# Products of constants that nobody reads, placed on TensorE in its waits at block ends and block heads

## The reference, cut to what matters

```python
# layer 1: state space and gated linear attention, then a gated MLP (2816 hidden)
x = x + ssd_gla_layer(rms_norm(x, ...), w_in, ..., w_out)
x = x + swiglu(rms_norm(x, ...), w_gate, w_up, w_down)
# layer 2: latent attention, then a gated MLP
x = x + mla_layer(rms_norm(x, ...), ...)
x = x + swiglu(rms_norm(x, ...), ...)
# layer 3: hgrn2_mix and retention_mix over one projection, gates, then the experts
x = x + merged @ w_out
x = x + peer_ffn(rmsnorm(x, ...), w_q, sub_keys, expert_u, expert_v)   # 16384 experts
return rmsnorm(x, final_norm_w)
```

## Time and profile before

| | us |
|---|---|
| median of 3 runs | 3814.06 (3812.29 to 3815.13) |
| the profiled execution's own time | 3814.17 |
| its span, first to last instruction | 3812.3 |
| PE busy | 3602.6, 94% of the span |
| DVE, POOL, ACT busy | 1951.2, 1615.7, 1392.0 |
| mean granted clock of PE | 0.974 of full speed |

### The profile page before, as it was taken

How to read it: one execution, slowest core, us unless ns; L and a number is a source line. 1 busy time by engine, 2 the same in 40 slices (tenths; PEclk the granted TensorE clock), 3 DMA queues, 4 the chain that set the end, 5 groups by cost and what they waited for, 6 DMA issues and landing times. The chain is left out here.

```text
span 3812.3 us, 50272 instructions
## 1 busy us (share of the span) xinstructions
PE 3602.6 (94%) x17241; PEld 2991.6 (78%) x17241; DVE 1951.2 (51%) x3519; ACT 1392.0 (37%) x2156; POOL 1615.7 (42%) x838
## 2 busy tenths in 40 slices
PE   8899899998999999998899999999999999999998
PEld 6667678786677878787687777779999999788886
DVE  6724333204552330127516122358899991787886
ACT  3333332224553222221211332333348994333334
POOL 4344354344205434441243344445786776422221
PEclk9999999999999999999999999999999999999999
DMA  5123133222003322220123122234878997999996
GB/s 164 39 81 94 39 95 98 87 95 93 23 18 94 99 89 92 83 92 24 40 93 95 55 83 81 86 102 139 266 242 292 379 383 265 365 361 348 343 343 229
DMA packets 274589, 580.13 MB, mean 152 GB/s; under 512 B 119648, under 2 KB 153824, under 8 KB 273040
## 3 DMA queue, kind: packets, MB, share of 16 engines
q1 hardware_dynamic: 237584, 444.07, 35.4%
q0 software_dynamic: 36864, 134.23, 10.1%
HBM read 523.66 MB, written 54.56 MB: 152 GB/s over the span
## 5 line engine op out<-in xcount | busy, mean ns | idle before, releaser
L425 PE MATMUL ps<-h_hi,w_hi 128*128 128x512 f32 x1880 | 752.3, 400 | 59.1 <-DVE h_lo L355 31.5
L426 PE MATMUL ps<-h_lo,w_hi 128*128 128x512 f32 x1880 | 743.3, 395 | 0.0
L427 PE MATMUL ps<-h_hi,w_lo 128*128 128x512 f32 x1880 | 742.4, 395 | 0.0
L572 POOL TENSOR_TENSOR w_lo<-ring,w_hi 128x1024 fp32r<-128x1024 f32 (+1 forms) x172 | 443.9, 2581 | 659.1 <-ACT w_hi L537 659.1
L425 PEld LDWEIGHTS ps<-h_hi,w_hi 128*128 128x128 f32 x1880 | 359.8, 191 | 157.4 <-issue 45.5
L537 ACT CAST w_hi<-ring 128x1024 fp32r<-128x1024 f32 (+1 forms) x172 | 191.1, 1111 | 743.1 <-PE ps L427 718.7
L426 PEld LDWEIGHTS ps<-h_lo,w_hi 128*128 128x128 f32 x1880 | 360.6, 192 | 75.5 <-issue 2.2
L427 PEld LDWEIGHTS ps<-h_hi,w_lo 128*128 128x128 f32 x1880 | 360.0, 191 | 76.2
L3305 POOL TENSOR_TENSOR w_lo<-ring,w_hi 128x1024 fp32r<-128x1024 f32 x142 | 359.0, 2532 | 141.2 <-ACT w_hi L3180 139.9
L3180 ACT CAST w_hi<-ring 128x1024 fp32r<-128x1024 f32 x270 | 283.1, 1049 | 371.1 <-PE ps L427 305.5
L3356 PE MATMUL ps<-h_hi,w_hi 128*128 128x384 f32 (+1 forms) x1152 | 401.9, 349 | 7.6 <-DVE h_lo L355 6.1
(11 more groups left out here) (424 smaller groups left out, 6748.5 us busy)
## 6 DMA issues: line engine op xcount, KB each, us to landing
ring<-in_expert_u SPq DMA_DIRECT2D x128, 512.0 KB
ring<-in_expert_v SPq DMA_DIRECT2D x128, 512.0 KB
ring<-in_w_gate_up SPq DMA_DIRECT2D x88, 512.0 KB
acts<-expert_gelu SPq DMA_DIRECT2D x128, 192.0 KB
gates<-peer_region SPq DMA_DIRECT2D x48, 512.0 KB
peer_region<-acts SPq DMA_DIRECT2D x128, 192.0 KB
peer_region<-gates SPq DMA_DIRECT2D x128, 192.0 KB
ring<-in_w_down SPq DMA_DIRECT2D x32, 704.0 KB
```

Of the source, the lines that this page charges most:

```text
L425: pe.matmul(out, w_hi, x_hi, start=start, stop=False)
L426: pe.matmul(out, w_hi, x_lo, start=False, stop=False)
L427: return pe.matmul(out, w_lo, x_hi, start=False, stop=stop)
L572: pool.tensor_tensor(half(c.w_lo, s), raw(s), half(c.w_hi, s).bitcast(F32), ALU.subtract).then_inc(c.lo_done.sem, 1)
```

## The change

A helper `occupy` issues n products of the constant table: the unit matrix stationary, the three constants (384 columns) moving, plain float32, into a PSUM bank that is free. Nothing reads what they write. They stand in 25 places, 82 products in all: at the head of a `linear` whose first piece waits for its input, at the end of four `linear` blocks (`rest`), at the end of `linear_tokens` and of the MLP's first block, at the head of the MLP, of the latent attention and of the expert block, ahead of the last sum of squares in the gated linear attention, and at three waits of the expert block. Where the bank could still be in use, a wait on `bank_free` or on a copy stands ahead of them, and in the expert block the wait for `chosen_made` moves behind two other waits and the products.

```diff
+def occupy(c, pe, bank, n):
+    for _ in range(n):
+        pe.matmul(c.ps[:, bank, 0:3 * P], c.ident, c.basic[:, 0:3 * P], start=True, stop=True)
...
             if src or normal:
+                pe.wait_ge(c.bank_free.sem, c.bank_free.at(1))
+                occupy(c, pe, 0, 3)
                 one(0, 0, 0, 0, 0, first=True)
             pieces(one, None if root_of or more else pe.Fori, 1 if src or normal else 0)
+            if rest:
+                pe.wait_ge(c.bank_free.sem, c.bank_free.at(1 + nb))
+                occupy(c, pe, nb % 2, rest)
             if root_of:
...
             pieces(one, pe.Fori)
+            pe.wait_ge(c.bank_free.sem, c.bank_free.at(1 + nb * NCH))
+            occupy(c, pe, 0, 3)
...
                     if h:
                         sum_squares(h - 1)
+                occupy(c, pe, 3, 4)
                 sum_squares(H - 1)
...
-        linear(c, d["w_small"], DT, 1, hh, hl, low_rank, then=first_pieces(d["w_ssd"][8:20]),
+        linear(c, d["w_small"], DT, 1, hh, hl, low_rank, then=first_pieces(d["w_ssd"][8:20]), rest=4,
                normal=lambda k: c.col("mix_norm_even", k), width=0)
...
-                               more=(state.sync, state.tensor, None))
+                               more=(state.sync, state.tensor, None), rest=3)
...
                     pe.wait_ge(c.bank_free.sem, c.bank_free.at(1))
+                    occupy(c, pe, 0, 3)
                     for k in range(DT):
                         normal.ready(pe, k)
...
                     with pe.Fori(1, pairs) as p:
                         for m in range(4):
                             piece(p, m)
+                    pe.wait_ge(c.bank_free.sem, c.bank_free.at(1 + HT))
+                    occupy(c, pe, 0, 3)
...
                 def first_latents():
+                    occupy(c, pe, 0, 3)
                     pe.wait_ge(c.lo_done.sem, split_at(0))
...
-                       more=(lambda sp, m: None, gated.tensor, gated.gpsimd), then=first_pieces(d["w_branch_ret0"]))
+                       more=(lambda sp, m: None, gated.tensor, gated.gpsimd), then=first_pieces(d["w_branch_ret0"]),
+                       rest=4)
...
-            linear(c, d["w_gates"], DT, 16, hh, hl, qk, beside=(merge.vector, merge.scalar), then=first_pieces(d["w_out_2"]))
+            linear(c, d["w_gates"], DT, 16, hh, hl, qk, beside=(merge.vector, merge.scalar), then=first_pieces(d["w_out_2"]),
+                   rest=4)
...
                 def gates(g):
+                    if g == 0:
+                        occupy(c, pe, 3, 3)
                     pe.wait_ge(hot_low_made.sem, hot_low_made.at(g + 1))
...
+                occupy(c, pe, 0, 3)
                 for m in range(NQ):
...
-                pe.wait_ge(chosen_made.sem, chosen_made.at(1))
                 pe.wait_ge(scores_kept.sem, scores_kept.at(NQ))
                 pe.wait_ge(x_kept.sem, x_kept.at(8))
+                occupy(c, pe, 2, 3)
+                pe.wait_ge(chosen_made.sem, chosen_made.at(1))
...
+                occupy(c, pe, SUM_BANK[0], 6)
                 for i in range(4):
                     add(i, i, first=i == 0)
```

More of the change, by code:

```diff
@@ L430, in linear, with linear_block @@
 def linear(c, w, kt, nb, hi, lo, dst, add=False, src=None, then=None, beside=None, root_of=None, normal=None,
-           width=D, more=None, ends=None, loads=()):
+           width=D, more=None, ends=None, loads=(), rest=0):
     with ExitStack() as ctx:
         linear_block(c, ctx, w, kt, nb, hi, lo, dst, add, src, then, beside, root_of,
-                     Normal(c, ctx, normal, width, None, ends, (hi, lo)) if normal else None, more, loads)
-def linear_block(c, ctx, w, kt, nb, hi, lo, dst, add, src, then, beside, root_of, normal, more, extra=()):
+                     Normal(c, ctx, normal, width, None, ends, (hi, lo)) if normal else None, more, loads, rest)
+def linear_block(c, ctx, w, kt, nb, hi, lo, dst, add, src, then, beside, root_of, normal, more, extra=(), rest=0):
     np_ = 1 if kt <= DT else 2
```

## The result

| | before | the change |
|---|---|---|
| median, us | 3814.06 (3812.08 to 3817.4, 5 runs) | 3793.12 (3790.42 to 3799.98, 5 runs) |
| ratio, 95% interval | | 0.9948 (0.9936 to 0.996) |
| profiled execution, its span | 3814.17, 3812.3 | 3792.65, 3790.9 |
| mean granted clock | 0.974 | 0.988 |

The change is faster by 20.9 us, 0.55%. The page's busy times answer to the earlier trace rows: PE has 164 records more and is busy 24.9 us longer, in a span that is 21.4 us shorter.

What follows compares the result with a forecast made beforehand. The prediction took TensorE, slowed by a low clock behind its waits, to bound the kernel: 3814.2 - 20.0 (eight places) - 1.5 (MLP heads) + 4.0 (new falls) = 3796.7 us, range 3780 to 3811, the forecast's own 3788 to 3804.

Steps and rivals of the forecast that it cites:

- What bounds the kernel: TensorE, busy in 94% of the span; its clock falls to 0.50 behind waits, losing half the busy time there.
- What the fill costs: All 82 products: 53 us of PE, 0.324 us per record, hidden in the waits; at full clock costed at nothing.
- rival (d): Slower: head fills at low clock end 1.61 us late; twelve heads 19.3 us, 3833, or half of them 3824; chance 0.09.
- The eight places: Eight low stretches behind filled one-piece waits, followed by dense streams: half of PE's busy time each, 20.0 us gained.
- The final sum: At the sum's head, 5.3 us of wait against 3.89 of fill; gain 5.30/2 = 2.65 us.
- Heads: Block heads with two waits, only the first filled: 1.5 us for the two MLP heads together, nothing for the others.
- Rival (a): The clock holds at heads too, behind six second waits: 13.9 us more, 33.9 us less in all, 3780; chance 0.07.
- Against: Falls that newly come at unfilled waits or reach further into dense work at heads: 4 us taken off the gain.
- The sum: The forecast total: 3814.2 - 20.0 - 1.5 + 4.0 = 3796.7 us, 0.45% less.
- Rival (c): Products with the unit matrix stationary don't count for the clock; it falls as before, fill hidden: 3814; chance 0.09.
- Rival (b): Half a hold: idle time left still brings falls in part of the eight; three holding gives 7.5 us, 3807; chance 0.15.

Runs made afterwards that it cites:

- e3: The change with fill products over only 16 of the 128 rows, same number and columns: 3810.34 us, ratio 0.9994.
- e8: The change with stationary data of 16 columns instead of 128 in every fill, all 128 rows: 3794.72 us, ratio 0.9953.
- e5: The change with six products instead of three at each of the twelve block heads: 3791.41 us, ratio 0.9947.
- e9_inner: The change plus fills in the heads' second waits and at three more places in or ending the latent attention block: 3788.12 us, ratio 0.9939.
- e1: The change without the 12 fills at block heads, the 13 others kept: 3797.2 us, ratio 0.9962.
- e4: The change plus fills of two to four products in the second waits of the heads: 3792.36 us, ratio 0.995.
- e6: The change with each fill cut (three products become one, four two, six three): 3804.13 us, ratio 0.9974.

## Why the prediction was right, and where it wasn't

- **What bounds the kernel**: right. The time is lost in PE's low clock behind waits. e3 and e8 are the proof: the same number of products at the same places, and stages gain where the clock held and not where it fell, at eight of eight places with 16 columns and at three (and half of a fourth) with 16 rows.
- **What the fill costs**: right in the change, nothing, at 0.30 us from record to record (3.65 us for twelve) where I had 0.324. But the reason at heads was too narrow. I had PE late by 1.61 us if the fill outlasts the first operand, and everything behind late too. e5 shows the second wait takes it up. With this rival (d) falls as priced. Fills did run at the low clock at three heads (3.14 us to the first triple at the first MLP's), and the stage behind gained 1.2 us all the same. Only with more products at such a head did the low clock cost something, 1.1 us in e5's first MLP and 1.8 in e9_inner's against the change.
- **The eight places**: the mechanism right at all eight, the size a fifth too large, 15.9 for 20.0. "Half of the busy time" holds where PE alone sets the pace: retention 1.47 for 1.51, w_down 2.74 for 3.03, final sum 2.25 for 2.65. It fails where PE at full clock runs into the next operand. In w_ssd's two parts and in w_out_2 PE now waits 0.77, 0.45 and 0.65 us for POOL's low half of a weight, and in the gate matrices 0.40 and 0.43 more for one-hot rows. There the lead grew by 3.1 us right behind the fill, nearly the 3.28, and 1.3 of it was lost again by the stage's end; in e1, where the clock held there too, all of it was lost, in waits for one-hot rows of up to 1.07 us. The term lacked a look at what stands next behind the stream. In the gated linear attention 2.86 for 1.70 hides a ninth place: the fill at the end of the values' product stands in a wait of 3.1 us, behind which before had a fall too (405.23 to 408.65), and I hadn't priced it. In e3, which has that fall still and not the one at the sum, the stage gains 1.37; so the sum itself gives less than the 1.70, and the ninth place some 1.5.
- **The final sum**: I had taken the 5.3 us wait as the one that the six products fill. It stands ahead of the fifth `add`, and the fill ahead of the first. The timeline after, at both:

```profile
3232.59 4.03 PE L287 MATMUL ps<-basic 128*128 128x384 f32 x12
...
3254.88 0.50 PE L431 MATMUL ps<-w_hi,one_hots 128*128 128x512 f32 x1 [1.46 <-DVE one_hots L3601]
```

  The fill ran 17 us early, pushed PE's work into the wait and shortened it from 5.26 to 1.46 us, 3.80, just its own length. It held the clock by making the wait shorter, at no cost since the wait ends with DVE's weights. The gain came as forecast, by a way that I had misread. That the order alone shows where the fill stands, and the trace which `add` waits, I had not put together.
- **Heads**: for the two MLP heads 1.5 was forecast and 1.55 measured, 1.3 of it by the fills. For the others 0 was forecast, and their stages grew by 1.9 in all; but without head fills (e1) they grew by 2.2, so the 0 stands for the heads themselves, and what the forecast lacked is the rest of these stages. Rival (a), 13.9 us more if the clock holds, didn't come, and e4 refutes its price: with no fall left behind the second waits the time was that of the change (ratio 0.995 for 0.9948), since the heads of the third layer's products are bound by low halves and what three other blocks gained was lost elsewhere.
- **Against**: wrong in sign. I took 4 us off for falls that come; one came (-1.6) and one went (+3.1).
- **The sum** with the measured terms: 3814.2 - 15.9 - 3.5 - 1.5 - 0.5 (start and values) = 3792.8, for 3792.65. The forecast was 4 us too high: the eight places 4.1 too much, the head stages 2.0 and the falls 5.5 too little, 0.5 not counted. That it was near is partly luck: the first of these errors goes against the others.
- **Rival (c)**, products by the unit matrix don't count: refuted by the eight windows at 1.00. The Trainium skill, TensorE: Matmul & The Clock Gate, section Part 4: PE-mode transpose, speaks of the transpose mode alone, and isn't to be widened to plain products with that operand: no run here tests the mode itself.
- **Rival (b)**, half a hold, didn't come with the change, but is real: e6 with half of the fill lies there.

What stays open: why the clock falls in some kernels and not in others at the same unfilled or half-used stretch (w_gla, and e3's eight places), what fills over more than 16 rows but not all would do, and whether e9_inner's 6.7 us hold, of which its trace shows 6.1 in the latent attention and the product behind it, part of it lost again at the MLPs' heads.

## What to carry to other kernels

Where one engine is busy nearly all the time, look at its clock in small windows before looking for work to remove; a wait costs its own length and, behind it, half of the dense work at the low clock. Fill a wait of such an engine with work over all 128 rows of the array, which held the clock at all eight places in the change, as much as ends before the wait does. Look also for products of the kernel's own that use few rows. At a block's head a fill that runs over by 1.4 us cost nothing where the next operand is made without PE, and 1.1 to 1.8 us where it ran at the low clock; at a block's end it delays the step by what it runs over.

What a held clock gives back is half of the busy time only if nothing else limits the stream right behind. Look which operand PE meets next: behind an input that is normed tile by tile it was in most blocks the low half made by DVE or POOL, and there the clock was worth nothing.

## What the runs showed of the hardware that I had not expected

- Products over 16 of 128 rows, as long and as many, left the clock to fall at five of eight places and gained nothing in all (3810.34 us, 28 low stretches), while products with 16 of 128 stationary columns held it at all eight (3794.72 us, 17).
- A product of constants whose stationary side is mostly zeros (the unit matrix) holds the clock as real data does: 1.00 in all eight windows.
- Where the clock falls was the same at 18 of 20 places in two executions of one program, though the first operand from memory came at 5.3 us in one execution of the change and at 6.1 in the other.
- A fall can stand where PE never waits (w_gla, 91.19 us without and 94.30 with it): in eight of twelve executions it began in or within 0.7 us behind 3.7 to 4.5 us of products over 16 rows.
